# Second attention, probabilities times values: from one float32 product per query tile to three rounded products per pair of tiles

## What is computed

```python
def one_block(q_blk):      # 128 queries at a time
    s = jnp.einsum('bqhgd,bkhd->bhgqk', q_blk, k, ...) * (HEAD_DIM ** -0.5)
    p = jax.nn.softmax(s, axis=-1).astype(v.dtype)
    return jnp.einsum('bhgqk,bkhd->bqhgd', p, v)
```

## Time and profile before

| | |
|---|---|
| median of 3 runs | 1710.5 us (1708.74 to 1711.29) |
| the profiled execution | 1711.27 us, of which the span is 1708.8 us |
| PE busy over the span | 1671.6 us, 98% |
| DVE busy | 1153.9 us, 68% |
| ACT busy | 890.8 us, 52% |
| POOL busy | 614.5 us, 36% |
| this attention's loop on PE | from 733.3 us to 879.2 us of the span |

### The profile page before, as it was taken

How to read it: one execution, slowest core, us unless ns; L and a number is a source line. 1 busy time by engine, 2 the same in 40 slices (tenths; PEclk the granted TensorE clock), 3 DMA queues, 4 the chain that set the end, 5 groups by cost and what they waited for, 6 DMA issues and landing times.

```text
span 1708.8 us, 24534 instructions
## 1 busy us (share of the span) xinstructions
PE 1671.6 (98%) x8633; PEld 1364.1 (80%) x8633; DVE 1153.9 (68%) x1730; ACT 890.8 (52%) x1552; POOL 614.5 (36%) x667
## 2 busy tenths in 40 slices
PE   8999999989999999999999999999999999999998
PEld 6878788767787667878888888888888878888886
DVE  5578685687457854376658747866733388586779
ACT  4465665787366754366542344565423364445453
POOL 2644445425542115311124432333244641515150
PEclk9999999999999999999999999999999999999999
DMA  7452633332321003201148621121133350515131
GB/s 222 117 181 85 188 91 119 90 99 74 90 89 41 26 13 89 62 26 31 33 135 273 197 62 38 42 58 50 50 87 98 98 163 23 185 32 177 55 118 50
DMA packets 216895, 160.55 MB, mean 94 GB/s; under 512 B 8078, under 2 KB 190359, under 8 KB 216791
## 3 DMA queue, kind: packets, MB, share of 16 engines
q1 hardware_dynamic: 193054, 108.72, 22.5%
q10 hardware_dynamic: 23736, 50.44, 8.6%
HBM read 156.98 MB, written 2.16 MB: 93 GB/s over the span
## 4 chain that ended last, share of the span: by engine, by line
PE 59%; issue 15%; DVE 11%; POOL 7%; ACT 6%; DMA 1%; ACTq 0%; POOLq 0%; DVEq 0%; SPq 0%
PE ps L664 14%; PE ps L668 14%; PE ps L665 14%; POOL wl L614 7%; PE ps L2333 2%; DVE mod_late L2729 2%; PE ps L2315 2%; PE ps L1681 1%; PE ps L2322 1%; PE ps L2879 1%; ACT wh L627 1%; PE ps L1713 1%; PE ps L1701 1%; DMA raw<-w_mlp 1%; PE ps L2845 1%
## 5 line engine op out<-in xcount | busy, mean ns | idle before, releaser
L614 POOL TENSOR_TENSOR wl<-raw,wh 128x256 fp32r<-128x256 f32 (+1 forms) x647 | 591.4, 945 | 997.8 <-ACT wh L627 997.7
L664 PE MATMUL ps<-ah,wh 128*128 128x512 f32 (+1 forms) x1144 | 457.5, 400 | 4.9 <-DVE al L792 2.2
L668 PE MATMUL ps<-ah,wl 128*128 128x512 f32 (+1 forms) x1144 | 447.4, 391 | 0.2
L665 PE MATMUL ps<-al,wh 128*128 128x512 f32 (+1 forms) x1144 | 446.2, 390 | 0.0
L627 ACT ACTIVATE wh<-raw 128x1024 fp32r<-128x1024 f32 (+1 forms) x188 | 196.8, 1048 | 188.2 <-PE ps L668 142.2
L664 PEld LDWEIGHTS ps<-ah,wh 128*128 128x128 f32 (+1 forms) x1144 | 214.0, 187 | 57.8 <-issue 7.2
L668 PEld LDWEIGHTS ps<-ah,wl 128*128 128x128 f32 (+1 forms) x1144 | 213.7, 187 | 49.4 <-POOL wl L614 1.9
L665 PEld LDWEIGHTS ps<-al,wh 128*128 128x128 f32 (+1 forms) x1144 | 214.2, 187 | 44.1 <-issue 1.7
L664 PE MATMUL ps<-bh,wh 128*128 128x512 f32 (+1 forms) x332 | 133.7, 403 | 0.7 <-DVE bl L1516 0.5
L668 PE MATMUL ps<-bh,wl 128*128 128x512 f32 (+1 forms) x332 | 129.9, 391 | 0.1
L665 PE MATMUL ps<-bl,wh 128*128 128x512 f32 (+1 forms) x332 | 129.7, 391 | 0.0
(11 more groups left out here) (500 smaller groups left out, 3308.2 us busy)
## 6 DMA issues: line engine op xcount, KB each, us to landing
raw<-w_in SPq DMA_DIRECT2D x52, 512.0 KB, 3.8
raw<-ssm_w_in SPq DMA_DIRECT2D x40, 512.0 KB, 3.9
ada_late<-w_ada ACTq DMA_DIRECT2D x16, 1024.0 KB, 6.8
raw<-w_mlp SPq DMA_DIRECT2D x32, 512.0 KB, 4.0
quarters<-w_mlp ACTq DMA_DIRECT2D x16, 1024.0 KB, 6.5
ada_raw<-w_ada ACTq DMA_DIRECT2D x16, 512.0 KB, 4.5
cum_rows<-cum_saved ACTq DMA_DIRECT2D x16, 512.0 KB, 3.9
raw<-ssm_w_out SPq DMA_DIRECT2D x16, 512.0 KB, 3.4
```

Source lines behind the costliest of these rows:

```text
L614: nc.gpsimd.tensor_tensor(wl[:, s, part], raw[:, s, part], wh[:, s, part].bitcast(F32), ALU.subtract).then_inc(lo_ready, LOW_PIECES * (par ...
L664: nc.tensor.matmul(dst, w_hi[k], x_hi[k], start=k == 0, stop=False)
L665: nc.tensor.matmul(dst, w_hi[k], x_lo[k], start=False, stop=False)
L668: ins = nc.tensor.matmul(dst, w_lo[k], x_hi[k], start=False, stop=k == n - 1)
```

## The change

Only the functions of this attention are changed.

1. Values: ACT rounds them to `v_hi` (`high_v`, three copies of 128x512 from PSUM), and DVE subtracts to `v_lo` (`take_v`, three subtractions). Before, DVE copied them.
2. Scaling of the probabilities: DVE makes only the reciprocal (`divide`), and ACT multiplies (`scale`, an Identity with the reciprocals as scale).
3. Turned probabilities: ACT's `copy_turned` rounds to `g_turned_hi`, one half of a buffer that is 256 queries wide, and DVE makes the remainder `g_turned_lo` from the same PSUM banks (`low_turned`). The next `turn_probs` waits for `low_turned`.
4. Products: `outputs(m)` handles two tiles at once, with 18 rounded matmuls of 256 columns, and needs both tiles' remainders.
5. PE's order: `outputs` of the pair before goes ahead of `turn_probs(n)` in even rounds, `sum_q` goes behind the turn, and of the query projection at `t == 3` two of three chunks go behind the turn.
6. ACT's and DVE's orders: see the loops below. `scale_q` of ACT is cut in two, `turn_q` moves from `t == 3` to the next head's `t == 0`, the two `gained` go to `t` = 1 and 2, one in each.
7. The buffer of squares, `p_sq`, moves onto a buffer of the norms, and `v_lo` onto another.

```diff
@@ pe_gqa
             def turn_probs(n):
                 pe.wait_ge(sem("g_probs_ready"), n + 1)
-                pe.wait_ge(*((sem("g_copied"), n) if n else (sem("k_ln"), KVH)))
+                pe.wait_ge(*((sem("g_lowered"), V_PARTS + n) if n else (sem("k_ln"), KVH)))
...
-            def outputs(n):
-                j, t = divmod(n, TT)
-                pe.wait_ge(sem("g_copied"), n + 1)
-                if t == 0:
+            def outputs(m):
+                j, two = divmod(m, TT // 2)
+                pe.wait_ge(sem("g_copied"), V_PARTS + 2 * m + 2)
+                pe.wait_ge(sem("g_lowered"), V_PARTS + 2 * m + 2)
+                if two == 0:
                     pe.wait_ge(acc_free[1], ACC0["gqa"][1] + 1 + j + 1)
-                v = slice(j // QPK * HD, (j // QPK + 1) * HD)
+                v, dst = slice(j // QPK * HD, (j // QPK + 1) * HD), bank(1)[:, two * PAIR:(two + 1) * PAIR]
                 for k in range(KT):
-                    ins_ = nc.tensor.matmul(bank(1)[:, t * P:(t + 1) * P], v_tok[:, k, v], g_probs_t[:, n % 2, k], start=k == 0, stop=k == KT - 1)
+                    nc.tensor.matmul(dst, v_hi[:, k, v], g_turned_hi[:, k], start=k == 0, stop=False)
+                    nc.tensor.matmul(dst, v_lo[:, k, v], g_turned_hi[:, k], start=False, stop=False)
+                    ins_ = nc.tensor.matmul(dst, v_hi[:, k, v], g_turned_lo[:, k], start=False, stop=k == KT - 1)
                 ins_.then_inc(sem("g_o"), 1)
...
                 if n + 1 < NQ:
                     scores(n + 1)
+                early = PROJECT[t][:1] if t == TT - 1 else PROJECT.get(t, ())
+                if t in PROJECT and j + 2 < QH:
+                    project_q(j + 2, early)
+                elif n in GATE_AHEAD:
+                    branch_gate_ahead(GATE_AHEAD[n])
+                if n and n % 2 == 0:
+                    outputs(n // 2 - 1)
+                turn_probs(n)
                 if t == 0 and j + 1 < QH:
                     sum_q(j + 1)
-                if t in PROJECT and j + 2 < QH:
-                    project_q(j + 2, PROJECT[t])
-                elif n in GATE_AHEAD:
-                    branch_gate_ahead(GATE_AHEAD[n])
-                turn_probs(n)
-                if n:
-                    outputs(n - 1)
-            outputs(NQ - 1)
+                if t == TT - 1 and j + 2 < QH:
+                    project_q(j + 2, PROJECT[t][1:])
+            outputs(NQ // 2 - 1)
@@ act_gqa
+            def scale(n):
+                act.wait_ge(sem("g_divided"), n + 1)
+                act.wait_ge(sem("g_exp"), n + 1)
+                nc.scalar.activation(g_probs[:, n % 2], g_probs[:, n % 2], ACT.Identity, scale=g_rinv[:, n % 2:n % 2 + 1]).then_inc(sem("g_probs_ready"), 1)
...
             for n in range(NQ):
                 j, t = divmod(n, TT)
+                if t == 3:
+                    copy_turned(n)
+                if n + 1 < NQ:
+                    exp(n + 1)
                 if t == 1 and j:
                     high(j - 1)
-                if n + 1 < NQ:
-                    exp(n + 1)
+                if t < 2:
+                    copy_turned(n)
                 if t == 0 and j + 1 < QH:
                     scale_q(j + 1)
                 if t == 3 and j + 2 < QH:
                     take_q(j + 2)
-                copy_turned(n)
+                if n + 1 < NQ:
+                    scale(n + 1)
+                if t == 0 and j + 1 < QH:
+                    root_q(j + 1)
...
-                if t == 2 and j + 1 < QH:
-                    split_ahead(act, "gqa", 0, q_unit(j + 1))
-                if t == 3:
+                if t == 2:
+                    copy_turned(n)
+                    if j + 1 < QH:
+                        split_ahead(act, "gqa", 0, q_unit(j + 1))
                     stack_high(j)
@@ dve_gqa
+            def low_turned(n):
+                dve.wait_ge(sem("g_copied"), V_PARTS + n + 1)
+                half = slice(n % 2 * P, (n % 2 + 1) * P)
+                nc.vector.tensor_tensor(g_turned_lo[:, :, half], ps[:, 6:8].rearrange("p b n -> p (b n)")[:, 0:TA].rearrange("p (k n) -> p k n", n=P),
+                                        g_turned_hi[:, :, half].bitcast(F32), ALU.subtract).then_inc(sem("g_lowered"), 1)
...
             for n in range(NQ):
                 j, t = divmod(n, TT)
-                if t == 1 and j:
-                    low(j - 1)
+                if t:
+                    low_turned(n - 1)
                 if n + 1 < NQ:
                     top(n + 1)
+                if t == 0 and 0 < j < QH - 1:
+                    turn_q(j + 1)
+                if t == 1 and j:
+                    low(j - 1)
                 if t == 2 and j + 1 < QH:
                     low_q(j + 1)
+                if t == TT - 1:
+                    low_turned(n)
                 if n + 1 < NQ:
-                    scale(n + 1)
+                    divide(n + 1)
                 if t == 0 and j + 1 < QH:
                     turned_q(j + 1)
                 if n == TT + 1:
                     low_k(1)
                 if t == 1 and j + 1 < QH:
                     scale_q(j + 1)
-                if t == 3 and j + 2 < QH:
-                    turn_q(j + 2)
-                if t == 3 and j < QH // 2:
-                    gained(dve, 2 * j)
-                    gained(dve, 2 * j + 1)
-                elif t == 3 and j < QH // 2 + 2:
+                if t in (1, 2) and j < QH // 2:
+                    gained(dve, 2 * j + t - 1)
+                elif t == 2 and j < QH // 2 + 2:
                     stack_low(j - QH // 2)
```

More of the change, by code:

```diff
@@ L2103, in _build @@
         k_feat = r("k_feat", [P, KVH, TA])
-        v_tok = r("v_tok", [P, KT, KVH * HD])
-        p_sq = r("p_sq", [P, TA])
-        p_rstd = r("p_rstd", [P, TA])
+        v_hi, v_lo = r("v_hi", [P, KT, KVH * HD], F32R), at("v_lo", [P, KT, KVH * HD], F32R, norm_v_at)
+        p_sq = at("p_sq", [P, T], F32, norm_sq_at)
+        p_rstd = r("p_rstd", [P, T])
         p_cos = r("p_cos", [P, T])
@@ L2424, in exp, with high_v @@
                                      bias=g_nmax[:, n % 2:n % 2 + 1], accum_out=g_rsum[:, n % 2:n % 2 + 1]).then_inc(sem("g_exp"), 1)
+            def scale(n):
+                act.wait_ge(sem("g_divided"), n + 1)
+                act.wait_ge(sem("g_exp"), n + 1)
+                nc.scalar.activation(g_probs[:, n % 2], g_probs[:, n % 2], ACT.Identity, scale=g_rinv[:, n % 2:n % 2 + 1]).then_inc(sem("g_probs_ready"), 1)
             def copy_turned(n):
                 act.wait_ge(sem("g_turned"), n + 1)
-                if n >= 2:
-                    act.wait_ge(sem("g_o"), n - 1)
-                nc.scalar.activation(g_probs_t[:, n % 2].rearrange("p k n -> p (k n)"), ps[:, 6:8].rearrange("p b n -> p (b n)")[:, 0:TA],
+                if n >= 2 and n % 2 == 0:
+                    act.wait_ge(sem("g_o"), n // 2)
+                nc.scalar.activation(g_turned_hi[:, :, n % 2 * P:(n % 2 + 1) * P],
+                                     ps[:, 6:8].rearrange("p b n -> p (b n)")[:, 0:TA].rearrange("p (k n) -> p k n", n=P),
+                                     ACT.Copy).then_inc(sem("g_copied"), 1)
+            def high_v(part):
+                act.wait_ge(*((sem("gv_projected"), part + 1) if part < 2 else (unit_done, unit("gqa", 0, 1) + 1 + CREDIT)))
+                nc.scalar.activation(v_hi[:, 2 * part:2 * part + 2], bank((6, 7, 3)[part]).rearrange("p (t d) -> p t d", t=2),
                                      ACT.Copy).then_inc(sem("g_copied"), 1)
             def high(j):
-                act.wait_ge(sem("g_o"), TT * (j + 1))
+                act.wait_ge(sem("g_o"), TT // 2 * (j + 1))
                 nc.scalar.activation(bh[:, j], bank(1), ACT.Copy).then_inc(sem("g_high"), 1)
@@ L2460, in act_gqa @@
                 split_ahead(act, "gqa", 0, half)
+            for part in range(3):
+                high_v(part)
             take_q(0)
@@ L2464, in act_gqa @@
             scale_q(0)
+            root_q(0)
             take_k(1)
@@ L2548, in take_v @@
             def take_v(part):
-                dve.wait_ge(*((sem("gv_projected"), part + 1) if part < 2 else (unit_done, unit("gqa", 0, 1) + 1 + CREDIT)))
-                nc.vector.tensor_copy(v_tok[:, 2 * part:2 * part + 2], bank((6, 7, 3)[part]).rearrange("p (t d) -> p t d", t=2)
-                                      ).then_inc(sem("gv_taken"), 1)
+                dve.wait_ge(sem("g_copied"), part + 1)
+                two = slice(2 * part, 2 * part + 2)
+                nc.vector.tensor_tensor(v_lo[:, two], bank((6, 7, 3)[part]).rearrange("p (t d) -> p t d", t=2), v_hi[:, two].bitcast(F32),
+                                        ALU.subtract).then_inc(sem("g_lowered"), 1)
+            def low_turned(n):
[3 more added lines that the diff above has]
+                                        g_turned_hi[:, :, half].bitcast(F32), ALU.subtract).then_inc(sem("g_lowered"), 1)
             def top(n):
```

26 lines of the change are left out of this document (14 added, 12 removed).

## The result

| | before | changed |
|---|---|---|
| median | 1710.2 us (7 runs, 1708.7 to 1713.8) | 1718.4 us (7 runs, 1715.6 to 1720.6) |
| profiled execution | 1711.27 us, span 1708.8 | 1715.56 us, span 1713.1 |
| PE busy | 1671.6 us | 1664.9 us |

The changed kernel takes 1.0044 times as long as the one before, with a 95% interval of 1.0034 to 1.0053: 7.5 us more (5.8 to 9.1). The median lies just inside the upper edge of the forecast's own range, 1712.8 to 1718.5.

The account below looks back on a forecast made before the run. PE was taken to bound the attention loop. Its work falls 6.1 us and new waits add 11.0, so +4.9 us: profiled execution 1711.27 to 1716.2, median 1710.5 to 1715.4 us; range 1707.0 to 1719.5.

Parts of the forecast that it names:

- the forecast's own range: Median of the changed kernel, 1712.8 to 1718.5 us, allowing 0.1 us error in remainder or copy plus the pair's price.
- The products: Attention loop on PE: rounded pairs at 2.14 us replace float32 outputs; PE's work falls by 6.1 us.
- The handover: From one turn's start to the next via ACT's copy and DVE's remainder: 2.72 us, remainder 0.95 us.
- The nine waits of the turn: PE before turns: 0.25 us in 7 heads, twice in the last, 2.2 us together; round 31, 0.7 us.
- Outputs: PE waits before outputs at t = 2 for the remainder of t = 1, DVE standing in line: together 6.1 us.
- The wait before the last pair: Loop's end: PE has nothing between the last turn and the last pair, a 2.1 us wait.
- The start: Loop's start: ACT's scaling delays the first turn 0.3 us and `sum_q` follows it; net loss 0.5 us.
- The sum of these: Whole loop: 6.1 us less PE work against 11.0 us of new waits, +4.9 us.
- the fall of the clock: Rival, loop's start: PE's 3.2 us idle stretch halves the clock, costing 4 us, so 1719.4 us; chance 0.03.
- the mid-loop waits are slack: Rival: remainder and turn chains overlap better, only start and end waits remain; -4.1 us, 1706.4 us; chance 0.14.
- only heads 6 and 7 wait: Rival: of the mid-loop waits only those where PE has least work remain; +0.6 us, 1711.1 us; chance 0.22.
- ACT did not become the bound: Rival that it would: copy and remainder 0.15 us dearer each, chain 3.0 us; +8.9 us, 1719.4 us; chance 0.12.

## Why the forecast was right, and where it was short

- *The products.* Forecast 2.14 us a pair. Where the clock is full, nine pairs measured 2.11 to 2.14 and six behind a wait 2.19 to 2.20, together as forecast. The rows of the scores and of the values' projection priced it. The estimate of 1.97 us a pair from the Trainium skill, "TensorE: Matmul & The Clock Gate", section "Wait — 56ns, not 53.3ns?", was too low.
- *The handover.* Forecast 2.72 us from turn to turn, measured 2.80; the remainder 0.955 us, forecast 0.95. The nine waits of the turn: eight of 0.25 and one of 0.60, forecast 0.25 and 0.7.
- *Outputs.* Forecast waits of 1.8, 0.45, 0.45, 1.85, 1.6 us in rounds 6, 10, 14, 26 and 30; measured 1.77, 0.38, 0.37, 1.77, 1.42, and the 0.25 in round 28, which the forecast had put before the turn. (The two sums that it sets against each other for rounds 10 and 14, 5.75 and 5.23, differ by 0.52 and not by 0.45.) The wait before the last pair: forecast 2.1, measured 1.99.
- *The start.* 3.20 us before the first turn; the scaling on ACT took 0.93 us where I had 0.84 to 0.90. From the last matmul of the scores to the first of the projection it is 6.10 us, 5.64 in the kernel before, so a loss of 0.46 us; forecast 0.5.
- *The sum of these.* Forecast +4.9 us; the loop without the fallen clock is 152.2 - 1.8 - 145.9 = 4.5 us longer. The runs say that the chain is the cause: without the remainder the waits go, shortened by 0.4 us it gives back what the layout said, and DVE's queue ahead of it accounts for rounds 6, 10 and 14.
- *What failed is the step on the clock.* I named the fall of the clock as a rival, for the start alone, gave it 0.03, and put it at nothing in the sum, because the rows of before show 1.00 through the start. Two things were wrong with that. First, my rows on the clock are those of the loop's start and of the span's end; the same profile has the two falls in other stages that are shown above, behind waits of 2.50 and 0.98 us. Second, one execution with 1.00 does not say that the clock holds there. It fell at the start in seven of nine profiles in which the 3.2 us wait stands unfilled, at a price of 1.3 to 2.4 us from the turn to the projection behind it (the rival had 4 us), and also in the one with the scaling alone on ACT, where the gap is in two pieces as before. At the loop's end it fell in four of the five profiles that have the wait of 2.0 us (the changed kernel twice, the one with products behind, the one without pairs, but not the one with moved work), and with pairs the last one then took 3.7 to 4.0 us; in halves, where the wait is 1.6 us, it did not fall. I had asked only whether `high` and `low` stay hidden there, and not what three rounds with short work and three waits do to the clock.
- *What that step was worth.* 4.5 us of waits and about 3 us of clock make the 7.5 us. The 3 us are an estimate. The mean clock of the changed kernel's executions is 0.9959, that of the kernel before 0.998 in each of the three series, and 0.002 of a span of 1713 us is 3.4 us where PE is busy.
- *What was luck.* The forecast's own range was made wide for errors of 0.1 us in copy and remainder, which did not come. That its upper edge, 1718.5, still takes in the median of 1718.4 is luck: the clock filled the room that was left for something else.
- *The other rivals.* That the mid-loop waits are slack, or that only heads 6 and 7 wait, is refuted by the waits themselves. ACT did not become the bound: copying into a half of the wide buffer took 0.81 us against 0.80, and in one head of the middle DVE and ACT have 13.4 and 14.1 us of work, where the forecast had 14.5 and 16.

How much of the 3 us belongs to which gap is argued from single profiles. Filling the end alone moved no median. Filling start and end came out at 5.0 us above the kernel before (3.1 to 6.8), where the changed kernel's two series have 7.5 (5.8 to 9.1) and 8.2 (5.8 to 10.6). These intervals overlap a little, so in time the gain of 2 to 3 us is likely and not shown. The mean clocks lie further apart: 0.997 to 0.999 in its seven executions, 0.994 to 0.998 in the twelve of the changed kernel.

## What to carry to other kernels

Where an engine is busy all the time, less work on it buys nothing by itself: lay the new chain between its instructions beside the work that it still has there, and look at the rounds with the least of it (the first, the last, and those in which another product is missing). A step that splits a result in two belongs in two parts as well, and work that seems free to move into a gap may be the cover of something else, a table load among it. A wait on TensorE, here of 1 to 3 us, can have a second price, the clock behind it, which falls in some executions and not in others. One profile may miss it, so look through the whole span of the trace for such falls before you call them unlikely in one place.

## What the runs showed of the hardware

- TensorE's clock fell to 1.2 GHz behind waits of 0.98 to 3.2 us, and behind a pair of waits of 1.22 and 0.85 us. It stayed low for about 3.5 us in most cases, 7 us at the changed kernel's end and at the start of two other versions, and 10.4 us twice in the version without pairs. It fell in some executions of one and the same kernel and not in others: the timed executions of the changed kernel in its first series have mean clocks from 0.994 to 0.997 over the span, and spans of 1713.1 to 1718.3 us, the longest with the lowest clock. The Trainium skill, "TensorE: Matmul & The Clock Gate", section "Why this matters for your kernels", advises against long idle gaps between bursts of matmuls. The falls behind the 3.2 us agree with that; those behind 2 us and less show that here a gap need not be long.
- A rounded matmul with new weights costs 0.228 us for 512 columns, 0.118 for 256, and still 0.110 for 128. With new weights for each, there is next to nothing to save below 256 columns.
- ACT's Identity on 128x768 with a pointer as its scale took 0.937 us, where the rounding copy without one took 0.842. That the pointer makes the difference, and not the function or the type, no run here separates.
